# Rotary half turn of queries and keys: eight-row SBUF to SBUF transfers in place of full-precision matmuls

## What is computed

```python
def partial_rotary(t, cos, sin):
    half = ROT_DIM // 2                     # ROT_DIM = 16 of HEAD_DIM = 64
    t1, t2, rest = t[..., :half], t[..., half:ROT_DIM], t[..., ROT_DIM:]
    return jnp.concatenate([t1 * cos - t2 * sin, t2 * cos + t1 * sin, rest], axis=-1)
...
        qa = partial_rotary(qa.reshape(b, s, 2 * N_HEADS_DIFF, HEAD_DIM), cos, sin)
        ka = partial_rotary(ka.reshape(b, s, 2 * N_HEADS_DIFF, HEAD_DIM), cos, sin)
...
        oa = diff_attention(qa, ka, va, lam)
        oa = rms_norm(oa, diff_sub_g[l]) * (1.0 - lam_init)
```

## Time and profile before

| | us |
|---|---|
| median of three runs | 2121.92 |
| the profiled execution, its own time | 2123.0 |
| its span in the profile | 2121.1 |
| PE busy | 2072.8 (98% of the span) |
| DVE busy | 1036.2 (49%) |
| ACT busy | 810.8 (38%) |
| POOL busy | 247.1 (12%) |
| mean granted TensorE clock | 0.996 |

### The profile page before, as it was taken

How to read it: one execution, slowest core, us unless ns; L and a number is a source line. 1 busy time by engine, 2 the same in 40 slices (tenths; PEclk the granted TensorE clock), 3 DMA queues, 4 the chain that set the end, 5 groups by cost and what they waited for, 6 DMA issues and landing times.

```text
span 2121.1 us, 25763 instructions
## 1 busy us (share of the span) xinstructions
PE 2072.8 (98%) x10471; PEld 1679.3 (79%) x10471; DVE 1036.2 (49%) x1872; ACT 810.8 (38%) x1543; POOL 247.1 (12%) x276
## 2 busy tenths in 40 slices
PE   7999999999999999999999999999999999999998
PEld 6767788888888767788888888878766788888887
DVE  6464454334436364454334436746556445433443
ACT  4355452222234355452222225344456334222222
POOL 2004410000002004310000002000267000000000
PEclk9999999999999999999999999999999999999999
DMA  5433333233322312233233332422321224323321
GB/s 157 119 65 74 97 103 99 96 95 99 94 90 76 100 50 67 81 97 100 95 94 100 95 95 57 114 62 79 87 60 31 85 90 124 100 90 100 100 95 65
DMA packets 269513, 189.42 MB, mean 89 GB/s; under 512 B 18156, under 2 KB 239524, under 8 KB 269396
## 3 DMA queue, kind: packets, MB, share of 16 engines
q1 hardware_dynamic: 264080, 174.28, 28.1%
q0 software_dynamic: 5168, 13.47, 2.6%
q10 hardware_dynamic: 148, 0.04, 0.0%
HBM read 183.53 MB, written 4.23 MB: 89 GB/s over the span
## 4 chain that ended last, share of the span: by engine, by line
PE 92%; DVE 4%; ACT 2%; POOL 1%; issue 1%; DMA 0%; DVEq 0%; ACTq 0%; POOLq 0%
PE bank L635 53%; PE bank L681 9%; PE bank L683 9%; PE bank L682 9%; PE bank L770 3%; PE bank L737 2%; PE bank L756 2%; PE bank L694 1%; PE bank L865 1%; DVE weights_hi_lo L1035 1%; PE bank L867 1%; PE bank L866 1%; ACT arena L1761 1%; PE bank L742 1%; DVE h_features L1073 1%
## 5 line engine op out<-in xcount | busy, mean ns | idle before, releaser
L635 PE MATMUL bank<-h_features,weights_hi_lo 128*128 128x512 f32 (+1 forms) x5088 | 1115.9, 380 | 5.1 <-DVE weights_hi_lo L1035 4.2
L635 PEld LDWEIGHTS bank<-h_features,weights_hi_lo 128*128 128x128 f32 x5088 | 916.8, 189 | 188.7 <-issue 6.4
L1035 DVE TENSOR_TENSOR weights_hi_lo<-weights,weights_hi_lo 128x1024 fp32r<-128x1024 f32 (+2 forms) x337 | 396.5, 1181 | 491.8 <-ACT weights_hi_lo L1702 491.1
L1702 ACT ACTIVATE weights_hi_lo<-weights 128x1024 fp32r<-128x1024 f32 (+2 forms) x337 | 337.8, 1007 | 276.3 <-PE bank L683 250.8
L681 PE MATMUL bank<-weights_hi_lo,hidden 128*128 128x512 f32 x528 | 205.8, 390 | 0.0
L683 PE MATMUL bank<-weights_hi_lo,hidden 128*128 128x512 f32 x528 | 205.4, 389 | 0.0
L682 PE MATMUL bank<-weights_hi_lo,hidden 128*128 128x512 f32 x528 | 205.4, 389 | 0.0
L1818 ACT ACTIVATE arena<-arena 128x512 f32<-128x512 f32 x66 | 41.7, 632 | 269.7 <-DVE arena L1194 269.7
L2173 POOL TENSOR_SCALAR arena<-arena,row_stats 128x256 f32<-128x256 f32 (+5 forms) x140 | 127.6, 924 | 139.6 <-DVE row_stats L1118 63.7
L1194 DVE TENSOR_TENSOR arena<-bank,arena 128x512 f32<-128x512 f32 x66 | 69.5, 1053 | 118.4 <-PE bank L635 110.9
L1821 ACT ACTIVATE hidden<-arena 128x512 fp32r<-128x512 f32 x66 | 41.7, 632 | 218.4 <-DVE arena L1200 218.4
(11 more groups left out here) (354 smaller groups left out, 2122.2 us busy)
## 6 DMA issues: line engine op xcount, KB each, us to landing
weights<-in_w_in_dram SPq DMA_DIRECT2D x78, 512.0 KB, 3.9
weights<-in_w_gate_dram SPq DMA_DIRECT2D x66, 512.0 KB, 3.8
weights<-in_w_up_dram SPq DMA_DIRECT2D x66, 512.0 KB, 3.9
weights<-in_w_down_dram SPq DMA_DIRECT2D x60, 512.0 KB, 3.6
weights<-in_w_out_dram SPq DMA_DIRECT2D x24, 512.0 KB, 3.6
bias_rows<-decay_scratch POOLq DMA_DIRECT2D x16, 256.0 KB, 4.6
weights<-in_w_in_dram SPq DMA_DIRECT2D x13, 256.0 KB, 3.2
weights<-in_w_down_dram SPq DMA_DIRECT2D x12, 256.0 KB, 2.6
```

Source lines behind the costliest of these rows:

```text
L635: last = e.matmul(out_ap, l, r, start=(j == 0), stop=(j == len(pairs) - 1))
L1035: e.tensor_tensor(pair_view(i, 1), raw_view(i), pair_view(i, 0).bitcast(F32), ALU.subtract).then_inc(done, tick(("split", i)))
L1702: e.activation(pair_view(i, 0), raw_view(i), ACT.Copy).then_inc(done, tick(("hi", i)))
```

## The change

Three of the four operations stay. The matmul goes; in its place ACT, right behind its copy into `ROPE`, waits for its own copy to end and issues four transfers of 8 rows x 512 columns (16 KB each) from `ROPE` to `HALF_TURN`: rows 8 to 15 go to 0 to 7, and rows 0 to 7 to 8 to 15, for each of the two heads of the tile. `HALF_TURN` is the fourth tile of the fox queries and keys, which is free until step 25. POOL clears both once in a layer (in the second layer it first waits for the last matmul of the layer before), since the other 96 rows are multiplied too. `crossed` waits for 64 more counts of a semaphore of its own, one for queries and one for keys. The sign moves into the sine table: frequencies of rows 0 to 7 of a head are negative. The matrix leaves the constants, which shrink from 897 to 769 columns.

```diff
-K_ID, K_ROT, K_TRI, K_MASK, K_FREQ, K_HOT = 0, 128, 256, 768, 896, 897
-NCONST = 897
+K_ID, K_TRI, K_MASK, K_FREQ, K_HOT = 0, 128, 640, 768, 769
+NCONST = 769
...
-            c[m, K_FREQ] = freq[m % 8]
+            c[m, K_FREQ] = freq[m % 8] if m % HD >= 8 else -freq[m % 8]
...
+        half_turn_in = [sem("queries_half_turn_arrival"), sem("keys_half_turn_arrival")]
...
+        HALF_TURN = [QB[:, 3, :], KB[:, 3, :]]
...
-                    def rotate(c, m):
-                        out_ap = bank((s, "rot", c, m))
-                        pe.wait_ge(act.done, act[s, "rope", c, m])
-                        e.matmul(out_ap[:, :], CST[:, K_ROT:K_ROT + P], ROPE[0 if c == C_QA else 1], start=True, stop=True
-                                 ).then_inc(done, tick((s, "rot", c, m)))
-
                     feature_tile((s, "qk", C_QA), HT)
                     feature_tile((s, "qk", C_KA), HT)
-                    rotate(C_QA, 0)
-                    rotate(C_KA, 0)
...
                     def fill(at):
-                        if at - 1 in FILL_AT and FILL_AT[at - 1][0] in (C_QA, C_KA):
-                            rotate(*FILL_AT[at - 1])
...
                         dve.wait_ge(done, dve[s, "straight", c, m])
-                        e.tensor_tensor(tmp, full((s, "rot", c, m))[:, :], SIN[:, :], ALU.mult).then_inc(done, tick())
-                        banks.leave(dve, (s, "rot", c, m))
+                        dve.wait_ge(half_turn_in[which], 64 * (N_DIFF * layer + m + 1))
+                        e.tensor_tensor(tmp, HALF_TURN[which], SIN[:, :], ALU.mult).then_inc(done, tick())
                         settle()
...
                         banks.leave(act, (s, "qk", c + m * P))
+                        act.wait_ge(pool.done, pool[s, "half turns cleared"])
+                        settle()
+                        for r0 in (0, HD):
+                            for to, at in ((0, 8), (8, 0)):
+                                e.dma_start(HALF_TURN[which][r0 + to:r0 + to + 8, :], ROPE[which][r0 + at:r0 + at + 8, :]
+                                            ).then_inc(half_turn_in[which], 16)
...
+                    if layer > 0:
+                        pool.wait_ge(pe.done, pe[f"L{layer - 1}", "down", NCHUNK - 1, 1, NT - 1])
+                    for rows in HALF_TURN:
+                        e.memset(rows, 0.0).then_inc(done, tick((s, "half turns cleared")))
```

More of the change, by code:

```diff
@@ L70, in shape_constants @@
     c[:, K_ID:K_ID + P] = np.eye(P)
-    for m in range(P):
-        if m % HD < 8:
-            c[m + 8, K_ROT + m] = -1.0
-        elif m % HD < 16:
-            c[m - 8, K_ROT + m] = 1.0
     k = np.arange(P)[:, None]
@@ L1290, in crossed @@
                         dst, tmp = (QA, ROPE[0]) if c == C_QA else (KA, ROPE[1])
+                        which = 0 if c == C_QA else 1
                         dve.wait_ge(done, dve[s, "straight", c, m])
-                        e.tensor_tensor(tmp, full((s, "rot", c, m))[:, :], SIN[:, :], ALU.mult).then_inc(done, tick())
-                        banks.leave(dve, (s, "rot", c, m))
+                        dve.wait_ge(half_turn_in[which], 64 * (N_DIFF * layer + m + 1))
+                        e.tensor_tensor(tmp, HALF_TURN[which], SIN[:, :], ALU.mult).then_inc(done, tick())
                         settle()
@@ L1848, in rope @@
                             act.wait_ge(dve.done, dve[s, "qk", c, m - 1])
-                        e.activation(ROPE[0 if c == C_QA else 1], bank[:, :], ACT.Copy, scale=SCALE if c == C_QA else 1.0
+                        which = 0 if c == C_QA else 1
+                        e.activation(ROPE[which], bank[:, :], ACT.Copy, scale=SCALE if c == C_QA else 1.0
                                      ).then_inc(done, tick((s, "rope", c, m)))
                         banks.leave(act, (s, "qk", c + m * P))
+                        act.wait_ge(pool.done, pool[s, "half turns cleared"])
[4 more added lines that the diff above has]
+                                            ).then_inc(half_turn_in[which], 16)
                     splits_for((s, "qk", C_QA))
```

## The result

The changed kernel takes 2151.7 us (median of 4, 2149.0 to 2152.2) against 2122.1 us of the kernel before, run beside it (median of 4, 2121.4 to 2124.8): a ratio of 1.0135, with a 95% interval from 1.0123 to 1.0148. It is 29.6 us slower. The forecast was 2122.6 us with a range up to 2130.0, so the prediction is wrong, and even its slower rival was too mild.

What follows compares the result with a forecast made beforehand. PE, busy 98% of the span, was taken as the bound. Gains of 2.7 us against 3.4 us of half clock gave 2123.7 from the profiled 2123.0, or 2122.6 us as a median; range 2114.5 to 2130.0.

Steps and rivals of the forecast that it cites:

- slower rival: Rows late, DVE stands in `crossed`, clock falls behind tile 2 too: 2126.0 us, or 2132.0 at 4.3 us; chance 0.22.
- Tile 0: Both rotations ahead of the value slabs go: 1.8 us gained in layer 1, 0.7 us in layer 0.
- The issues on ACT: Four issues behind each copy hold ACT 1.6 us, 0.40 us each, and cost nothing because ACT idles there.
- The landing: Transfer lands 2.05 us after its issue; sine product 3.3 us behind the copy's end, bounds 2.5 and 4.35 us.
- The queries' 0.9 us: Queries' rotation on PE at tiles 1 to 3 of each layer: its removal gains the full 0.9 us each.
- Tile 1, the scores of step 4: PE waits for key tile 1's sum: scores 1.2 us later, wait about 3.0 us, net -0.3 us per layer.
- Tiles 2 and 3: Each layer: queries gain 0.9 us, sine product 0.7 us later before the product with the values, net +0.2 us each.
- The clock: PE's clock halves for 3.4 us after step 4's wait in both layers, costing 1.7 us each, 3.4 us in all.
- For it: in L0 POOL's strip too: Argument for the slower rival: in layer 0 POOL's strip of bias rows is also in flight; no size given.
- The last rival: Everything is hidden and all 14.4 us of the 16 rotations are gained: 2107.5 us; chance 0.02.

Runs made afterwards that it cites:

- issue only: Changed kernel, but ACT's 64 transfers go from constant rows to rows nobody reads and DVE waits for no arrival: 2116.6 us, ratio 0.9976.
- keys by matmul, strips late: Changed kernel with the keys rotated by matmul as before and layer 0's bias strips written behind the rotations: 2126.9 us, ratio 1.0018.
- no transfers: Changed kernel without the transfers and the wait for them, matmuls still gone, POOL's clears kept: 2116.5 us, ratio 0.9973.
- strips-late kernel: Changed kernel with layer 0's eight bias strips written at steps 16 to 30, behind the last rotation: 2143.0 us, ratio 1.0102.

## Why the prediction was wrong, point by point

- **Tile 0** (2.5 us to gain): right in kind. In the change's own trace layer 0's stretch begins 0.5 us sooner (0.7 forecast) and the part between the stretches is 1.1 us shorter (1.8); alone it gave 2.3 us. How it splits over the layers the two traces tell differently.
- **The issues on ACT** (1.6 us, "nothing"): 2.62 us. One issue is 0.63 us, not 0.40. The rows for it were loads out of DRAM; those out of SBUF are longer in every rotation here. Their cost on ACT is indeed nothing where nobody waits for ACT behind them (issue only: 2116.6 against 2116.5 us), and 3.5 us where PE does (keys by matmul, strips late).
- **The landing, the step that failed**: 3.3 us from copy to sine product, with an upper bound of 4.35; the measured distances in layer 1 are 4.0 to 5.8 us and in layer 0 up to 8.6. Two terms of it were too small. The fourth issue starts 2.0 us behind the first, not 1.2. And from its own start to the sine product the fourth transfer takes, in layer 1, 2.0 and 2.3 us for the queries of tiles 3 and 2, 3.1 for those of tile 1 and 2.7 to 3.7 us for the keys, for 2.05 forecast. Four in a row are not the reason for this second part: its last data packet ends 1.6 us behind its issue where no slab is under way, as at query tiles 2 and 3 of layer 1. Where one is, at the first two key tiles, it ends 3.0 and 2.3 us behind it, within 0.2 us of the slab's own last packet. Windows from the fourth issue to that packet, key tile 1 and query tile 2 (the last number is GB/s):

```profile
753.90:756.90 3.00, 0.30 (x1) 0.14 (x1) 1.34 (x5) 1.63 (x5) 0.00 (x0) 1.00 0.71 195
770.80:772.40 1.60, 1.60 (x9) 1.33 (x8) 0.21 (x2) 0.66 (x3) 0.00 (x0) 1.00 0.14 26
```

  That the slab is the cause is argued from these coincidences; no run moved it. The prediction had seen the slab and priced it by a middle value of 2.05 us, with 3.1 as its bound; four of the six key tiles 1 to 3 lay over that bound. It had no row for a strip in the way.
- **The queries' 0.9 us** (gained in full at six tiles): not so. With the queries by transfer and the keys by matmul three matmuls are gone from layer 1's stretch and it is as long as before (70.9 for 71.0 us). With all six gone and nothing to wait for it is 68.3 us: 2.7 us shorter, for matmuls of 5.7 us. DVE's order takes the rest.
- **Tile 1, the scores of step 4**: the mechanism is the one told, PE waits for the sum of key tile 1. The size was 3.0 us forecast, 4.6 measured.
- **Tiles 2 and 3** (+0.2 each): waits before the product with the values of 2.2 and 1.6 us were forecast and left without a fall of the clock; they are 4.2 and 2.7 us, and the clock falls.
- **The clock**: one fall per layer and 3.4 us were forecast. There are five stretches with 37.4 us at half clock, most of them 6.8 us long. The length of a wait, by which the prediction decided, does not tell the two apart: behind 1.75 us the clock was halved in one layer and whole in the other (no transfers), and behind the wait of 1.6 us of the earlier trace rows it is halved in the change (1482.0 to 1485.3 us, granted 0.50). What it costs was tested on the strips-late kernel alone: 9.9 us for 27.3 us fewer at half clock. For the change itself it was not tested; at the same ratio its 37.4 us come to 13.6 us, and half of PE's 25.7 busy us in them, 12.9 us, is the most that it can be. So, by this estimate, the term was too small by some 9 us.
- **The slower rival** named the mechanism that came about (DVE stands in `crossed`, the copy out of bank 7 is queued behind it, the clock falls behind tile 2), with 0.22, but had 2132.0 us for a landing of 4.3 us. Its six microseconds for each further one were too few: two transfers less, 1.3 us of issues, gave 17.7 us, 8.2 of them in layer 1 (82.2 to 74.0 us), where the rival had 3 for each. It counted three places per layer at full clock, without longer falls.
- **"For it: in L0 POOL's strip too"**: named and not priced. It is worth 8.7 us, in two of the three tiles; why not in the third the runs do not tell.
- **The last rival** (all hidden, 2107.5 us) cannot be reached: with no transfer and no wait at all it is 2116.5, and PE then waits 7.9 us for DVE.

## What to carry to other kernels

Before an engine's own step is replaced by a transfer, look at the engine that consumes the result: if it works through a fixed order, each arrival holds all that is queued there, and the slack to compare with is the slack of that engine's next dependants, not the transfer's share of the queues. Find the arrival that ends last ahead of the busiest engine, here the keys', and take the others' stands for nothing until a run says more. Count small transfers, since four on one queue are issued one behind another, and price each by a row of its own kind (source and destination, with or without a large transfer beside it) or give the range a long tail. Where PE's waits grow to some microseconds, add the half clock; on the strips-late kernel it was near half of the loss. A transfer pays only where a long stretch of unrelated work lies over it, as over tile 0.

## What the runs showed of the hardware that was not expected

- A transfer of 8 rows of 2 KB from SBUF to SBUF held ACT for 0.63 us per issue (the median of the 64; loads on the same queue at the start 0.24 to 0.37), also with the constants as the source. On POOL four took 2.0 us.
- The Trainium skill (DMA: Bandwidth & Descriptors, Specifications) gives a first byte after about 0.6 us for transfers of Scalar. In the trace of the change the first data packet of the first of four starts 0.64 or 0.65 us after its issue ends at 11 of the 16 places, mostly 1.28 us after it begins, and 1.2 to 2.2 us after its end at the others. Counted from the end of the issue the trace agrees with the page at those 11; counted from its start it does not.
- An issue on ACT's queue took 4.4 us twice, 1.2 and 0.7 us after POOL had finished issuing a write of 256 KB out of 8 rows of SBUF; a third such write, at the same place among four issues, lengthened none. With that write elsewhere none took over 0.76 us. What the two share there, the runs do not tell.
- In the two attention stages PE's clock came back after 6.8 us in four places and 10.2 us in one, where the trace before had 3.4 us each time. Waits of 1.6 and 1.75 us were followed by the whole clock in one place and by half of it in another. The runs do not show what sets either.
- The last data of four 16 KB transfers ended 1.6 us behind the last issue with no slab under way, and up to 3.2 us with one (key tile 1 of layer 0), within 0.2 us of the end of the slab's packets.
